# Moving the second layer's gate rows from the first output projection into the second input projection

## The reference, cut to what matters

```
s_lat = silu(c);  s_ctx = silu(c_ctx)
for l in range(2):
    shift,   scale,   gate   = split(s_lat @ w_mod[l] + b_mod[l], 3)
    shift_c, scale_c, gate_c = split(s_ctx @ w_mod[l] + b_mod[l], 3)
    hx = rmsnorm(x, norm_g[l]) * (1 + scale) + shift
    hc = rmsnorm(ctx, norm_g[l]) * (1 + scale_c) + shift_c
    ... = split(hx @ w_in[l])            # q, k, v, gates, pool, convolution inputs
    y = mix(...)                          # attention, pooling, 31-tap convolution
    if l == 0: ctx = ctx + gate_c * y_c
    x = x + gate * y                      # y already holds the product with w_out[l]
x = rmsnorm(x, final_g)
# second block: sh1, sc1, g1, sh2, sc2, g2 = split(silu(c_2) @ w_mod_2 + b_mod_2, 6), one layer
```

## Time and profile before

| | us |
|---|---|
| median of three executions | 2971.7 |
| lowest and highest | 2971.41, 2990.23 |
| the profiled execution, its own time | 2989.88 |
| its span, first to last instruction | 2988.1 |
| TensorE busy | 2867.4 |
| GpSimd busy | 1831.5 |
| VectorE busy | 1732.9 |
| ScalarE busy | 1453.6 |

### The profile page before, as it was taken

How to read it: one execution, slowest core, us unless ns; L and a number is a source line. 1 busy time by engine, 2 the same in 40 slices (tenths; PEclk the granted TensorE clock), 3 DMA queues, 4 the chain that set the end, 5 groups by cost and what they waited for, 6 DMA issues and landing times.

```text
span 2988.1 us, 48572 instructions
## 1 busy us (share of the span) xinstructions
PE 2867.4 (96%) x17809; PEld 2473.7 (83%) x17809; DVE 1732.9 (58%) x3203; ACT 1453.6 (49%) x2228; POOL 1831.5 (61%) x756
## 2 busy tenths in 40 slices
PE   6799999999899799999989999999999999999999
PEld 4688887777778798878878999999978888888888
DVE  4487892799788857547667886652334444442000
ACT  3222223566522442248646887655446555555443
POOL 1244444333244584455576776778878888888997
PEclk9899999999999899999999999999999999999999
DMA  9876421555677697233594554445555666665555
GB/s 378 318 271 263 166 98 64 194 195 203 233 284 296 248 352 318 97 109 115 191 342 154 168 171 150 147 151 176 176 177 204 229 234 225 232 211 192 202 202 183
DMA packets 147414, 621.50 MB, mean 208 GB/s; under 512 B 16288, under 2 KB 17616, under 8 KB 126288
## 3 DMA queue, kind: packets, MB, share of 16 engines
q1 hardware_dynamic: 146128, 614.48, 57.5%
q10 hardware_dynamic: 1152, 5.24, 0.4%
HBM read 617.54 MB, written 2.12 MB: 207 GB/s over the span
## 4 chain that ended last, share of the span: by engine, by line
issue 46%; POOL 29%; PE 24%; POOLq 1%; DVE 0%; DVEq 0%
POOL w_low L691 29%; PE bank L726 16%; PE bank L727 8%; POOLq L686 0%; POOLq L690 0%; POOLq L691 0%; DVE region L1821 0%; DVE region L1824 0%; DVEq L1821 0%; POOLq L2655 0%
## 5 line engine op out<-in xcount | busy, mean ns | idle before, releaser
L691 POOL TENSOR_TENSOR w_low<-raw,w_high 128x1024 fp32r<-128x1024 f32 x752 | 1831.3, 2451 | 1145.3 <-ACT w_high L1198 1142.9
L1198 ACT ACTIVATE w_high<-raw 128x1024 fp32r<-128x1024 f32 x752 | 793.4, 1057 | 806.1 <-PE bank L739 300.6
L737 PE MATMUL bank<-h,w_high 128*128 128x256 f32 (+1 forms) x2816 | 947.1, 336 | 10.2 <-POOL w_low L691 7.1
L738 PE MATMUL bank<-h,w_high 128*128 128x256 f32 (+1 forms) x2816 | 933.7, 332 | 0.0
L739 PE MATMUL bank<-h,w_low 128*128 128x256 f32 (+1 forms) x2816 | 933.6, 332 | 0.0
L737 PEld LDWEIGHTS bank<-h,w_high 128*128 128x128 f32 x2816 | 535.4, 190 | 86.3 <-issue 19.0
L726 PE MATMUL bank<-h,w_high 128*128 128x512 f32 x1664 | 593.8, 401 | 8.9 <-POOL w_low L691 4.8
L738 PEld LDWEIGHTS bank<-h,w_high 128*128 128x128 f32 x2816 | 535.6, 190 | 50.5 <-issue 0.7
L739 PEld LDWEIGHTS bank<-h,w_low 128*128 128x128 f32 x2816 | 535.3, 190 | 50.6
L727 PE MATMUL bank<-h,w_low 128*128 128x256 f32 x1664 | 469.5, 282 | 0.0
L726 PEld LDWEIGHTS bank<-h,w_high 128*128 128x128 f32 x1664 | 315.2, 189 | 89.5 <-POOL w_low L691 6.1
(11 more groups left out here) (263 smaller groups left out, 3463.6 us busy)
## 6 DMA issues: line engine op xcount, KB each, us to landing
raw<-in_w_in SPq DMA_DIRECT2D x344, 512.0 KB, 3.8
raw<-in_w_up SPq DMA_DIRECT2D x176, 512.0 KB, 3.4
region<-in_w_rows SPq DMA_DIRECT2D x71, 1024.0 KB, 7.5
row_extra<-in_w_rows SPq DMA_DIRECT2D x57, 1024.0 KB, 6.7
raw<-in_w_out SPq DMA_DIRECT2D x96, 512.0 KB, 5.5
raw<-in_w_down SPq DMA_DIRECT2D x96, 512.0 KB, 3.4
row_extra<-in_w_half_rows SPq DMA_DIRECT2D x64, 512.0 KB, 4.4
region<-in_w_mods SPq DMA_DIRECT2D x28, 1024.0 KB, 9.9
```

The costliest lines, as they stand in the source:

```text
L691: nc.gpsimd.tensor_tensor(WL[s][:, part], RAW[s][:, part], WH[s][:, part], ALU.subtract) \
L737: nc.tensor.matmul(bank[:, 0:n], WH[slot][:, w], h, start=first and j == 0, stop=False)
L738: nc.tensor.matmul(bank[:, 0:n], WH[slot][:, w], l, start=False, stop=False)
L1198: return nc.scalar.activation(out, in_, func, **kw)
```

## The change

The 16 tiles of the second layer's gate (`mods[80:96]`) leave stage `out0` and form a new stage `gate1` of 18 rows (two vectors, 16 rows), numbered 34 to 51 behind the rows of `in1`. Stage `out0` falls from 36 rows to 20, with two instead of four before the first residual. The rows of `in1` and `gate1` are half rows: each 1 MB load holds two features' halves, and takes two sums of 1024 elements; `in1` so has a second vector (34 rows in all). `gate1` has two places in memory.

SyncE asks for one row per unit up to unit 19, then for 8 rows per 5 units, and for three more per unit after unit 32; its last row stands before unit 35. VectorE makes rows 18 to 32 between the taps of the convolution (one after every second tap), row 33 after the copies for the pooling, rows 34 to 38 between pooling offsets, and rows 39 to 51 after `cv_pool` is signalled and before it waits for `cv_sum`. The pooling sums move to banks 4 and 7, so that banks 5 and 6 can hold the vector; `conv_sum`, which writes bank 4, also waits for `cv_pool`, and `pool_product` waits for the gate rows.

```diff
-    ROW_STAGES = {... "out0": (ROW_OUT0, 36), "in1": (ROW_IN1, 33), "out1": ...}
+    ROW_GATE1 = [ROW_EXTRA[:], *r2(10240)]
+    ROW_STAGES = {... "out0": (ROW_OUT0, 20), "in1": (ROW_IN1, 34), "gate1": (ROW_GATE1, 18), "out1": ...}
-    out0_rows = lambda n: min(36, 4 + 9 * (n + 1) // 4)
+    out0_rows = lambda n: min(20, 2 + 5 * (n + 1) // 4)
...
         def row_in1(e):
-            if e == 0:
-                row_cond("in1", e, slice(2, 3))
+            if e >= 34:
+                if e % 9 == 7:
+                    row_cond("gate1", e - 34, slice(0, 1), (e - 34) // 9, 2)
+                else:
+                    row_load("gate1", e - 34, dram["w_rows"][64 + 8 * ((e - 34) // 9) + (e - 34) % 9 - 1])
+            elif e % 17 == 0:
+                row_cond("in1", e, slice(2, 3), e // 17, 2)
             else:
-                row_load("in1", e, dram["w_rows"][32 + e - 1])
+                row_load("in1", e, dram["w_rows"][32 + 16 * (e // 17) + e % 17 - 1])
...
-                    begin, plan = 4, [3 + 3 * max(0, t - 4) // 4 + 7 * max(0, t - 19) // 4 for t in range(28)]
-                    n_rows, row = 33, row_in1
+                    begin, plan = 4, [3 + max(0, min(t, 19) - 4) + 8 * max(0, t - 19) // 5 + 3 * max(0, t - 32) for t in range(36)]
+                    n_rows, row = 52, row_in1
...
         conv_sum:      pe.wait_ge(sem("cv_conv"), l + 1)
+            if l:
+                pe.wait_ge(sem("cv_pool"), l + 1)
         pool_product:  pe.wait_ge(sem("cv_pool"), l + 1)
+            if l:
+                pe.wait_ge(sem("row_out"), ROW_DONE["gate1"])
...
-        def small(l):
+        def small(l, rows=None):
-            pools = in_banks(1, 2) if l else [y[:, 0, :], *AUX[1:]]
+            pools = in_banks(0, 3) if l else [y[:, 0, :], *AUX[1:]]
             for turn, tap in ...:            # convolution
+                if rows and turn % 2:
+                    rows(18 + turn // 2)
...
+            if rows:
+                rows(33)
             for turn, off in ...:            # pooling
+                if rows and turn % 3 == 2:
+                    rows(34 + turn // 3)
...
             last.then_inc(sem("cv_pool"), 1)
+            for e in range(39, 52) if rows else ():
+                rows(e)
             dve.wait_ge(sem("cv_sum"), l + 1)
...
         def rows_in1(e):
-            row_sum(mod_col(95 + e, 2), place, place, 4, UNIT).then_inc(sem("row_used"), 1)
-            if e == 32:
-                row_bias(ROW_ALL["in1"], 96, 32, 2, 3).then_inc(sem("row_out"), 1)
+            gate = e >= 34
+            stage, e = ("gate1", e - 34) if gate else ("in1", e)
+            units, tile0, cond = (8, 80, 0) if gate else (16, 96, 2)
+            half, unit = e // (units + 1), e % (units + 1) - 1
+            ...
+            for r in range(2):
+                m = 2 * unit + r
+                weights = place[:, HALF * r:HALF * (r + 1)]
+                last = row_sum(mod_col(tile0 + m, cond) if half else ROW_PART[:, 32 * gate + m:32 * gate + m + 1],
+                               weights, weights, 5, HALF)
+            last.then_inc(sem("row_used"), 1)
+            if half and unit == units - 1:
+                row_bias(ROW_ALL[stage], tile0, 2 * units, cond, cond + 1, 32 * gate).then_inc(sem("row_out"), 1)
...
-                for e in range(9, 33):
+                for e in range(9, 18):
                     rows_in1(e)
-                small(1)
+                small(1, rows_in1)
...
-                for e in range(4):
+                for e in range(2):
                     rows_out0(e)
```

More of the change, by code:

```diff
@@ L96, in lay_out @@
     out["w_mods"] = mods[:32]
-    early, late = np.concatenate([mods[32:48], mods[64:80]]), np.concatenate([mods[48:64], mods[80:96]])
-    out["w_rows"] = np.concatenate([rows_of(early, 0, 2), rows_of(early, 1, 2), rows_of(mods[96:128]),
+    early = np.concatenate([mods[32:48], mods[64:80]])
+    out["w_rows"] = np.concatenate([rows_of(early, 0, 2), rows_of(early, 1, 2),
+                                    rows_of(mods[96:128], 0, 2), rows_of(mods[96:128], 1, 2),
+                                    rows_of(mods[80:96], 0, 2), rows_of(mods[80:96], 1, 2),
                                     rows_of(mods[128:144], 0, 2), rows_of(mods[128:144], 1, 2),
                                     rows_of(mods[176:192], 0, 2), rows_of(mods[176:192], 1, 2),
-                                    *(rows_of(late, q, 4) for q in range(4))])
+                                    *(rows_of(mods[48:64], q, 4) for q in range(4))])
     rows = rows_of(mods[144:176])
@@ L342, in build @@
     ROW_IN1 = [ROW_EXTRA[:], *r2(4096, 6144)]
+    ROW_GATE1 = [ROW_EXTRA[:], *r2(10240)]
     ROW_OUT1 = [ROW_EXTRA[:], *r2(0, 4096)]
     ROW_UP = [ROW_EXTRA[:]]
-    ROW_STAGES = {"in0": (ROW_IN0, 34), "att0": (ROW_ATT0, 64), "out0": (ROW_OUT0, 36), "in1": (ROW_IN1, 33), "out1": (ROW_OUT1, 18), "up": (ROW_UP, 18)}
+    ROW_STAGES = {"in0": (ROW_IN0, 34), "att0": (ROW_ATT0, 64), "out0": (ROW_OUT0, 20), "in1": (ROW_IN1, 34), "gate1": (ROW_GATE1, 18), "out1": (ROW_OUT1, 18), "up": (ROW_UP, 18)}
     ROW_FIRST, ROW_LANDED = {}, {}
@@ L530, in row_out0 @@
                 sp.wait_ge(sem("at_y"), 8)
-            if e % 9 == 0:
-                row_cond("out0", e, slice(0, 2), e // 9, 4)
+            if e % 5 == 0:
+                row_cond("out0", e, slice(0, 2), e // 5, 4)
             else:
-                row_load("out0", e, dram["w_rows"][96 + 8 * (e // 9) + e % 9 - 1])
+                row_load("out0", e, dram["w_rows"][112 + 4 * (e // 5) + e % 5 - 1])
         def row_in1(e):
-            if e == 0:
-                row_cond("in1", e, slice(2, 3))
+            if e >= 34:
[5 more added lines that the diff above has]
+                row_cond("in1", e, slice(2, 3), e // 17, 2)
             else:
-                row_load("in1", e, dram["w_rows"][32 + e - 1])
+                row_load("in1", e, dram["w_rows"][32 + 16 * (e // 17) + e % 17 - 1])
         def row_out1(e):
@@ L547, in row_out1 @@
             else:
-                row_load("out1", e, dram["w_rows"][64 + 8 * (e // 9) + e % 9 - 1])
+                row_load("out1", e, dram["w_rows"][80 + 8 * (e // 9) + e % 9 - 1])
         def row_up(e):
@@ L554, in row_up @@
             else:
-                row_load("up", e, dram["w_rows"][80 + 8 * (e // 9) + e % 9 - 1])
+                row_load("up", e, dram["w_rows"][96 + 8 * (e // 9) + e % 9 - 1])
         row_in0(0)
@@ L602, in stream @@
                 assert asked == n_rows
-                with sp.Fori(len(plan) // 2, 18) as i:
-                    two(i)
+                if l == 0:
+                    with sp.Fori(len(plan) // 2, 18) as i:
+                        two(i)
                 unit(9, 0)
@@ L625, in stream @@
                 for t in range(4, 17):
-                    plan = out0_rows(t - 4) + 1 if t < 16 else 36
+                    plan = out0_rows(t - 4) + 1 if t < 16 else 20
                     for e in range(asked, plan):
@@ L1886, in small @@
                 own.mark(V.tensor_copy(pools[g], up[:, g, :]))
-            for off in [o_ for h in range(8) for o_ in (-1 - h, h + 1)][:15]:
+            if rows:
+                rows(33)
+            for turn, off in enumerate([o_ for h in range(8) for o_ in (-1 - h, h + 1)][:15]):
                 groups = [g for g in range(4) if -(1 << g) <= off < (1 << g)]
@@ L2003, in rows_out0 @@
         def rows_out0(e):
-            q, unit = e // 9, e % 9 - 1
+            q, unit = e // 5, e % 5 - 1
             if unit < 0:
@@ L2009, in rows_out0 @@
             place = row_landed("out0", e)
-            def total(r, c):
+            weights = [place[:, QUARTER * r:QUARTER * (r + 1)] for r in range(4)]
+            for r, c in ((0, 0), (1, 0), (0, 1), (2, 0), (1, 1), (3, 0), (2, 1), (3, 1)):
                 n = 4 * unit + r
[L2014 to L2030, removed]
+                total = mod_col(48 + n, c) if q == 3 else ROW_PART[:, 32 * q + 2 * n + c:32 * q + 2 * n + c + 1]
@@ L2031, in rows_out0 @@
+                if c:
+                    own.wait(1 if r < 3 else 0)
+                last = row_sum(total, weights[r], weights[r] if c else ROW_OUT[:, QUARTER * (r % 2):QUARTER * (r % 2 + 1)],
+                               6 + c, QUARTER)
+                if c == 0:
+                    own.mark(last)
             last.then_inc(sem("row_used"), 1)
-            if e == 35:
+            if e == 19:
                 dve.wait_ge(sem("row_used"), ROW_ALL["out0"])
-                part = [ROW_PART[:, 48 * i:48 * (i + 1)] for i in range(3)]
+                part = [ROW_PART[:, 32 * i:32 * (i + 1)] for i in range(3)]
@@ L2035, in rows_out0 @@
                 for i in (1, 2):
                     seq(add(part[0], part[0], part[i]))
-                row_bias(ROW_ALL["out0"], 48, 16, 0, 2, 0)
-                row_bias(ROW_ALL["out0"], 80, 16, 0, 1, 32).then_inc(sem("row_out"), 1)
+                row_bias(ROW_ALL["out0"], 48, 16, 0, 2, 0).then_inc(sem("row_out"), 1)
```

(23 more changed lines are left out.)

## The result

The changed kernel is slower: 2985.47 us in the median of 20 executions (2975.58 to 2998.28) against 2972.14 for the kernel before on the same chip (20 executions, 2967.72 to 2990.23). The ratio is 1.0032, interval 1.0018 to 1.0046: 5 to 14 us lost where 3 were forecast to be gained. The profiled execution took 2981.74 us, its span is 2980.0.

What follows compares the result with a forecast made beforehand. TensorE, busy 96% of the span, was taken as the bound, so only its waits counted. Terms -8.3 - 9.3 + 6.0 + 8.5 = -3.1 us, carried to the median of 2971.7, gave 2968.6; range 2954 to 2984.

Steps and rivals of the forecast that it cites:

- Out0: Stage out0: removing 16 gate rows shortens two TensorE waits, gaining 17.6 us.
- the early wait: Early in out0, TensorE's wait for unit 4's low half: 6.3 us gained, 8.3 with the clock.
- the late one: End of out0, TensorE's wait for VectorE's last sum of squares: 4.0 us instead of 13.3, gaining 9.3.
- Early in1: Early in1: a row before every unit from 5 to 19 delays loads, costing 6.0 us.
- my loop: Early in1: load, halves, chunks, row, next row asked for; 14 us for two units against TensorE's 11.4.
- the full loop: Early in1: units 10 and 12 each lose the whole 2.6 us instead of the half taken.
- the upper end: Early in1: cost of 11 us, with the full loop and the clock falling.
- Tail: Rows 39 to 51 before the mean, 3.5 us each: conv_var 6.5 us late, costing 8.5 with the clock.
- the tail decides: Rival, chance 0.20: rows 39 to 51 hold VectorE longer past cv_sum; 2976 us, or 2985 at landings of 7.7.
- Costs taken as nothing: Convolution and pooling: rows 18 to 38 and conv_sum's new wait cost nothing; nor do pool_product's waits or row size.
- The DMA rate: Units 5 to 19: loads need 368 GB/s and fit; a limit near 358 would add 1.6 to 2 us.
- 334 GB/s as the bound of units 5 to 19: Rival, chance 0.05: DMA at 334 GB/s bounds these in1 units, 9 us in all; 2977 us.

Runs made afterwards that it cites:

- E6: Changed kernel with rows 3 to 17 of early in1 asked for one unit earlier; out0 to out1 took 851.0 us against 779.3 before, one execution.
- E1: Changed kernel with rows 3 to 17 of early in1 asked for one unit later; ratio to the kernel before 0.9972.
- E5: Changed kernel with E1's edit and a third place for gate rows, output not the reference's; ratio to the kernel before 0.9933.
- E7: E1 with more rows between convolution and pooling steps, leaving 7 instead of 13 behind cv_pool, still two places; ratio to the kernel before 0.9945.
- E2: Changed kernel with rows 47 to 51 moved behind the mean on VectorE; ratio to the kernel before 1.0013.
- E4: Changed kernel with the edits of E1 and E2 together; ratio to the kernel before 0.9966.
- E8: Changed kernel with only a third place for gate rows, output not the reference's; out0 to out1 took 774.9 us against 779.3 before, one execution.
- E3: Kernel before with the second layer's gate rows left out of out0 and made nowhere; ratio to the kernel before 0.9918.

## Why the prediction was wrong

It said 2968.6, a gain of 3.1, from four terms.

- **Out0, -17.6 forecast, -18.8 measured.** Right step by step: the early wait gone, the late one 3.2 where I had taken 4.0. VectorE's two additions took 2.05.
- **Early in1, +6.0 forecast, +14.2 measured. This step failed.** The mechanism was right, down to the round (14 forecast, 14.8 measured) and its end with the last chunks (the last two on VectorE start at 1058.19). But the step "I take half, since my loop adds up steps that partly overlap" had no row behind it, and the sum let the loss begin only at unit 8. Seven waits from 1018.68 to 1072.20 add to 12.45, one for nearly every unit from 6 to 13, and 1.7 us more go to a stretch at half clock. In the prediction's own terms: the full loop would have made 3.4 + 2 x 2.6 = 8.6, where these units wait for 9.1; units 6 and 7, whose five-microsecond delay was seen and given no price, wait for 3.3; and the 1.7 of half clock was left to the upper end. A loop of 14 us for two units against TensorE's 11.4 costs 1.3 for every unit while it lasts, from the first that it touches, and the measured 14.8 costs 1.7; E6, E1 and the kernel after show it. Even my upper end of 11 was below it.
- **Tail, +8.5 forecast, +13.0 measured. This step failed in size.** Row 39 came at 1227.87 (forecast 1234.6, from times of the kernel before, against which TensorE was by then 4.8 early: 1229.8), but a row took 3.72 instead of 3.5, so the wait was 10.0 instead of 6.5; behind it 3.0 of half clock instead of 2.0. I took the shortest landing of the earlier trace rows, 4.7, on the ground of low traffic, for a stretch in which units load as well: it moved 307 GB/s, not less than half of 415, and line 513 (the row loads) shows 4.9 at least and 5.4 in the median from 1195 to 1270 us. The rival "the tail decides" had put the balance at 5.2, and its sign was the one that came; but of the 10.5 us between my sum and the stretch the tail is 4.5 and the loop 8.2 (out0 and the rest take 2.2 back).
- **The rest** is 1.0 less than before; in out1, the wait for the last sum of squares is 3.4 us instead of 4.5, for a reason that is not shown. -18.8 + 14.2 + 13.0 - 1.0 = +7.4.
- **Costs taken as nothing.** Rows 18 to 38, `conv_sum`'s new wait and the half rows' size cost nothing, as forecast (E5, E7). `pool_product` cost nothing in the changed kernel, though not in E2 and E4.
- **The DMA rate.** 414 GB/s were moved from 1075 to 1100 us of the kernel after, and E1 moved 368 from 1025 to 1050 without a wait of TensorE. The limit of about 358 that I had weighed (the Trainium skill, DMA: Bandwidth & Descriptors, Where 436 GB/s comes from) does not bind here: the trace disagrees with it, at 414 GB/s on one core. Nor did the rival come that had 334 GB/s as the bound of units 5 to 19.

The range ended at 2984, 1.5 us short, since neither of the two costs had its full value in it. Of the 13.3 us between the medians, the stretch holds 7.4, which lies within the interval of 5 to 14; what the rest is, no run shows.

## What to carry to other kernels

When a queue issues loads in an order that depends on their use, write the loop down, and divide its round by the units that pass in it: above the bound engine's pace the whole difference is paid for every unit, below it nothing; one unit of slack was worth 15 us here. Rows with two places cost (landing + use) / 2 wherever the engine has nothing else to do (4.9 to 5.4 and 2.4 us give 3.65 to 3.9, against 3.72 measured), so put them between its other steps, as E7 did, and leave few for the end. Moving such work behind a result that is waited for helps only if the queue that feeds it has nothing urgent behind it: look for every engine that works in order and would meet the late load first, as ScalarE did in E4.

## What the runs showed of the hardware

**Two paces at one clock.** In the last stage (740 to 754 us of the same products, one after another) some executions are slower by 1.9% throughout, with the clock granted in full. The kernel before and after, 2400 to 2500 us:

```profile
2400.00:2500.00 100.00, 100.00 (x568) 86.76 (x567) 42.03 (x88) 57.30 (x88) 84.75 (x36) 1.00 0.64 221
```

```profile
2400.00:2500.00 100.00, 100.00 (x578) 87.46 (x578) 42.72 (x89) 58.38 (x92) 85.48 (x37) 1.00 0.66 226
```

568 products are recorded against 578; in the timelines they start 176.7 and 173.3 ns apart. That is 14 us over the stage. The profiles of E2, E4, E6, E7 and E8 are at the slower pace, those of E1, E3 and E5 at the faster. The kernels share this stage's work, and of the 20 executions of the kernel before, 11 lie between 2967 and 2973 us and 7 between 2983 and 2991, some 14 apart; so the pace most likely belongs to the execution and not to the kernel, but no kernel was profiled at both. It is one reason why E7's profiled execution (span 2966.1) is longer than E3's (2953.9) although its stretch is 1.9 us shorter. What sets the pace is open.

**Port.** VectorE's four products at 1.43 and at 5.58 us (E7 and E4, above) are the second surprise: the same instructions, slower by 4.15 us beside four halves of GpSimd that come back to back once their loads are late. That is the smaller part of E4's delay; the larger is ScalarE's late root.
